# The joint between an embedding gate and the next block's mixer, rearranged by halves of the tokens

## What is computed

```python
# end of the first block: gate by an embedding, then the block's last norm
gate = jax.nn.sigmoid(rms_norm(x, norm_ple) @ w_ple_gate)
x = x + gate * (p @ w_ple_proj)
x = rms_norm(x, norm_final)                       # x * rsqrt(mean(x*x) + 1e-6) * norm_final
# begin of the second block: its norm, modulated, and its mixer's projections
h = rms_norm_2(x, pre_mix_g) * (1.0 + sc1) + sh1
proj = h @ w_in                                   # first the attention's q (4 stripes), k, v
```

## Time and profile before

| | |
|---|---|
| median of 3 runs | 2946.78 us |
| the profiled execution | 2942.8 us, span 2941.0 us |
| TensorE busy | 2821.1 us, 96% |
| VectorE, ScalarE, GpSimd busy | 45%, 31%, 27% |
| mean granted TensorE clock | 0.988 |

### The profile page before, as it was taken

The page is one execution under the profiler, slowest core; times in us unless marked ns, Lnnn a source line. Parts: engine busy times, 40 slices in busy tenths (PEclk is TensorE's granted clock), DMA queues, the critical chain, the costliest instruction groups (busy, mean ns, idle before and its releaser), DMA issues.

```text
span 2941.0 us, 31529 instructions
## 1 busy us (share of the span) xinstructions
PE 2821.1 (96%) x12846; PEld 2261.9 (77%) x12846; DVE 1309.8 (45%) x1448; ACT 916.1 (31%) x1467; POOL 802.1 (27%) x428
## 2 busy tenths in 40 slices
PE   8999999999999999999999999888999999999996
PEld 6666678887788888888877777677767888888885
DVE  6777642231434434432443545326364343444436
ACT  6666421121311111111254233356352312222223
POOL 2433422223212221222243211123431222121224
PEclk9999999999999999999999999999999999999998
DMA  3000011122123222221112101011321111111113
GB/s 113 22 22 9 22 47 53 48 73 79 71 86 116 93 86 100 95 78 51 57 50 94 60 29 36 29 54 58 115 83 47 50 51 49 44 44 50 51 46 126
DMA packets 60864, 182.90 MB, mean 62 GB/s; under 512 B 6473, under 2 KB 15913, under 8 KB 60593
## 3 DMA queue, kind: packets, MB, share of 16 engines
q1 hardware_dynamic: 60720, 180.89, 17.8%
HBM read 165.61 MB, written 15.25 MB: 61 GB/s over the span
## 4 chain that ended last, share of the span: by engine, by line
PE 82%; DVE 5%; ACT 5%; issue 4%; POOL 2%; DMA 2%; SPq 0%; DVEq 0%; POOLq 0%; ACTq 0%
PE psum_mem L543 65%; PE psum_mem L579 2%; PE psum_mem L837 1%; PE psum_mem L842 1%; PE psum_mem L839 1%; PE psum_mem L614 1%; POOL w_lo L2833 1%; PE psum_mem L617 1%; PE psum_mem L615 1%; PE psum_mem L901 1%; PE psum_mem L1066 1%; PE psum_mem L643 1%; DVE left L2060 1%; PE psum_mem L867 1%; ACT w_hi L1203 1%
## 5 line engine op out<-in xcount | busy, mean ns | idle before, releaser
L2833 POOL TENSOR_TENSOR w_lo<-w_raw,w_hi 128x1024 fp32r<-128x1024 f32 (+1 forms) x233 | 549.0, 2357 | 1795.4 <-ACT w_hi L1203 1795.4
L543 PE MATMUL psum_mem<-h_hi,w_hi 128*128 128x512 f32 x2192 | 685.3, 394 | 23.2 <-DVE h_lo L1944 14.0
L543 PE MATMUL psum_mem<-h_hi,w_lo 128*128 128x512 f32 x2192 | 679.7, 391 | 12.0 <-POOL w_lo L2833 12.0
L543 PE MATMUL psum_mem<-h_lo,w_hi 128*128 128x512 f32 x2192 | 678.2, 391 | 0.0
L543 PEld LDWEIGHTS psum_mem<-h_hi,w_hi 128*128 128x128 f32 x2192 | 412.3, 189 | 115.7 <-issue 25.3
L543 PEld LDWEIGHTS psum_mem<-h_hi,w_lo 128*128 128x128 f32 x2192 | 412.3, 189 | 103.5 <-POOL w_lo L2833 18.0
L543 PEld LDWEIGHTS psum_mem<-h_lo,w_hi 128*128 128x128 f32 x2192 | 413.9, 189 | 87.6
L1203 ACT CAST w_hi<-w_raw 128x1024 fp32r<-128x1024 f32 (+1 forms) x233 | 234.0, 1005 | 658.2 <-PE psum_mem L543 511.4
L1949 DVE TENSOR_TENSOR tmp_mem<-psum_mem,norm_row 128x1024 f32<-128x1024 f32 x46 | 56.2, 1225 | 295.3 <-PE psum_mem L543 295.2
L2266 DVE TENSOR_TENSOR x_block<-x_block,psum_mem 128x1024 f32<-128x1024 f32 x88 | 107.4, 1220 | 67.7 <-PE psum_mem L543 65.1
L2876 POOL TENSOR_TENSOR beta<-beta,left 128x128 f32<-128x128 f32 (+2 forms) x96 | 86.8, 905 | 143.5 <-DVE left L2060 141.5
(11 more groups left out here) (355 smaller groups left out, 4006.7 us busy)
## 6 DMA issues: line engine op xcount, KB each, us to landing
ada_raw<-in_w_ada SPq DMA_DIRECT2D x48, 512.0 KB, 4.5
w_raw<-in_w_up_b SPq DMA_DIRECT2D x44, 512.0 KB, 3.3
w_raw<-in_w_in_a SPq DMA_DIRECT2D x32, 512.0 KB, 3.2
w_raw<-in_w_ffn_gate SPq DMA_DIRECT2D x22, 512.0 KB, 3.6
w_raw<-in_w_ffn_up SPq DMA_DIRECT2D x22, 512.0 KB, 3.6
w_raw<-in_w_ffn_down SPq DMA_DIRECT2D x22, 512.0 KB, 4.7
w_raw<-in_w_down_b SPq DMA_DIRECT2D x22, 512.0 KB, 3.2
w_raw<-in_w_in_b_ml SPq DMA_DIRECT2D x16, 512.0 KB, 4.1
```

The costliest lines, as they stand in the source:

```text
L543: made = e.matmul(pairs.half(use, half), wt, x[:, half_of(half)], start=at == 0 and part == 0, stop=at == len(rhs) - 1 and part == 2, skip ...
L2833: e.tensor_tensor(w_lo[:, i, 0:width], w_raw[:, i, 0:width], w_hi[:, i, 0:width].bitcast(F32), ALU.subtract).then_inc(*S.of("w_lo", c))
```

## The change

- Gate rows 0 to 5 stay as they are, but for "next" the squares are scaled by a new column, `final_gain` = sqrt(norm_final^2 + 1e-6), made by ScalarE (3 instructions on 128x8) and VectorE (4 such). So one sum serves both norms, and the step that joined two sums is gone. The plain sum is still made, for a later stage.
- Gate rows 6 and 7 run half by half: row 6 half 0, row 7 half 0, row 6 half 1, row 7 half 1. Everything behind them (scaling, sigmoid, embedding, add, square) is on 128x512 tiles.
- The sum for "next" is made in PSUM: three matmuls with ones for each half add `row2` (rows 0 to 5) and the squares of rows 6 and 7 up. Two of half 0's stand within row 6 half 1, the third behind it. Half 1's stand behind row 7 half 1, ahead of the projections.
- The finished norm is written to PSUM, over its sum, and read from there.
- `mix2` (normed row, `h_hi`, `h_lo`) is made for half 0 and then half 1, and `qk_at` 0 and 1 run over half 0 and then half 1, with `qk_at` 1 two groups behind.
- The fillers on constants (162 matmuls) are gone.
- The plain squares of rows 6 and 7 are made by ScalarE among half 1's `h_hi`, and added by VectorE after its last `h_lo`. SyncE stores `x1` 6 and 7 after three more weight loads instead of between them, and `plain_row` when that late sum is there.

```diff
+            def add_up(use, half, row, first, last):      # was further down, as was halved()
+                made = e.matmul(pairs.half(use, half), const("ones"), row[:, half_of(half)], start=first, stop=last, ...)
 # TensorE
-            for m in range(KD):
+            for m in range(6):
 ...
-            sum_partitions("next", row2, (("inv_m", ("next", 1)),), ("row_v", ("next", "both")), CLOCK_NORM)
+            ends = [take("w_pg") for _ in range(2)]
+            for m in (6, 7):
+                for _ in halved(("pg", m), ends[m - 6], 0, ple_half):
+                    pass
+            row = halved(("pg", 6), ends[0], 1, ple_half)
+            for at in range(KD):
+                next(row)
+                if at == 4:
+                    w.wait_ge("row_g", ("next", 5))
+                    add_up(sum_next, 0, row2, True, False)
+                    w.wait_ge("square", ("next", 6, 0))
+                    add_up(sum_next, 0, gate_sq[0], False, False)
+            w.wait_ge("square", ("next", 7, 0))
+            add_up(sum_next, 0, gate_sq[1], False, True)
+            for _ in halved(("pg", 7), ends[1], 1, ple_half):
+                pass
+            add_up(sum_next, 1, row2, True, False)
+            for m in (6, 7):
+                w.wait_ge("square", ("next", m, 1))
+                add_up(sum_next, 1, gate_sq[m - 6], False, m == 7)
-            two(("w_qk_at", "w_qk_at"), (("qk_at", 0), ("qk_at", 1)), h_rhs("mix2"),
-                ((("rope_in", 0),), (("rope_in", 1),)), CLOCK_NORM + 5)
+            for half in range(NH):
+                steps = [halved(use, n, half, ...) for use, n in firsts]
+                for k in range(KD):
+                    next(steps[0])
+                    if k >= 2:
+                        next(steps[1])
 ...
 # ScalarE
-            ahead(2)
-            w.wait_ge("row_v", ("final", 7))
-            inverse("next", row2, tmp[:, 1, :], eps=1)
+            unit()
+            for m in (6, 7):
+                gate_row(m, 0)
+                gate_square(m, 0)
+            logarithms()
+            inverse_half("next", 0, row2, gate_sq[0], 1)
+            unit()
+            gate_row(6, 1)
+            mix_row(0, 0)
+            gate_square(6, 1)
+            mix_row(1, 0)
             ahead(2)
+            gate_row(7, 1)
+            mix_row(2, 0)
+            gate_square(7, 1)
+            logarithms()
+            mix_row(3, 0)
+            inverse_half("next", 1, row2, gate_sq[0], 1)
+            for k in range(4, KD):
+                mix_row(k, 0)
             for k in range(KD):
+                mix_row(k, 1)
+                if k < 2:
+                    square("final", 6 + k, gate_sq[2 + k][:, :], x1[:, 6 + k, :])
 # VectorE
-            inverse("next", row2, tmp[:, 1, :], eps=EPS * EPS)
-            normed_to_h("mix2", x1, row2, lambda k: gain[:, k:k + 1], lambda k: mod[:, k:k + 1])
+            for m in (6, 7):
+                gate_scaled(m, 0)
+                gate_row(m, 0)
+            gate_scaled(6, 1)
+            inverse_half("next", 0, row2, gate_sq[0], EPS * EPS)
+            mix_normed(0, 0)
+            gate_row(6, 1)
+            mix_normed(1, 0)
+            mix_low(0, 0)
+            gate_scaled(7, 1)
+            mix_normed(2, 0)
+            mix_low(1, 0)
+            gate_row(7, 1)
+            for k in range(3, KD):
+                mix_normed(k, 0)
+                mix_low(k - 1, 0)
+            mix_low(KD - 1, 0)
+            inverse_half("next", 1, row2, gate_sq[0], EPS * EPS)
+            for k in range(KD):
+                mix_normed(k, 1)
+                if k > 0:
+                    mix_low(k - 1, 1)
+            mix_low(KD - 1, 1)
+            for m in (6, 7):
+                w.wait_ge("square", ("final", m))
+                e.tensor_tensor(plain_row[:, :], plain_row[:, :], gate_sq[m - 4][:, :], ALU.add)...
 # SyncE
-            for m in range(KD):
+            for m in range(6):
                 if m % 4 == 0:
                     unit()
                 unit()
+                park(m)
+            unit()
+            unit()
             ahead(2)
+            park(6)
+            park(7)
             unit(2)
             w.wait_ge("row_v", ("final", 7))
             e.dma_start(io["row_park"], plain_row[:, :])...
```

More of the change, by code:

```diff
@@ L575, in sum_partitions, with halved @@
                              skip_group_check=True).then_inc(*S.of("sum", (stage, half)))
+            def halved(use, n, half, rhs, blocks=range(KD)):
+                i, cols = n % 2, half_of(half)
+                for at, b in enumerate(blocks):
+                    high, low = w_hi[:, i, block_of(b)], w_lo[:, i, block_of(b)]
+                    x_high, x_low, events = rhs(at, half)
+                    for event in events:
+                        w.wait_ge(*event)
+                    for part, (wt, x) in enumerate(((high, x_high), (high, x_low), (low, x_high))):
+                        w.wait_ge("w_lo" if part == 2 else "w_hi", n)
+                        made = e.matmul(pairs.half(use, half), wt, x[:, cols], start=at == 0 and part == 0,
+                                        stop=at == KD - 1 and part == 2, skip_group_check=True)
+                    if at == KD - 1:
+                        made.then_inc(*S.of("full", use + (half,)))
+                    yield
+                unit_end[n] = ("full", use + (half,))
+            def add_up(use, half, row, first, last):
+                made = e.matmul(pairs.half(use, half), const("ones"), row[:, half_of(half)], start=first, stop=last,
+                                skip_group_check=True)
+                if last:
+                    made.then_inc(*S.of("sum", (use[1], half)))
             def turn(out, in_, rows=P):
@@ L792, in rotate @@
                 made.then_inc(*S.of("full", use))
-            two(("w_qk_at", "w_qk_at"), (("qk_at", 0), ("qk_at", 1)), h_rhs("mix2"),
-                ((("rope_in", 0),), (("rope_in", 1),)), CLOCK_NORM + 5)
+            h_mix2 = [(h_hi[:, k, :], h_lo[:, k, :],
+                       (("h_hi", ("mix2", k, 1)), ("h_lo", ("mix2", k, 1)))) for k in range(KD)]
+            firsts = [(("qk_at", s), take("w_qk_at")) for s in range(2)]
+            for use, _ in firsts:
+                for event in pairs.take(use, (("rope_in", use[1]),)):
+                    w.wait_ge(*event)
+            for half in range(NH):
+                steps = [halved(use, n, half, lambda k, half: (
+                    h_hi[:, k, :], h_lo[:, k, :],
+                    (("h_hi", ("mix2", k, half)), ("h_lo", ("mix2", k, half))))) for use, n in firsts]
+                for k in range(KD):
+                    next(steps[0])
+                    if k >= 2:
+                        next(steps[1])
+                for s in steps:
+                    for _ in s:
+                        pass
             for s in range(2, 5):
@@ L1053, in tensor @@
                     sum_partitions("plain", plain_back, (("inv_m", ("plain", 1)),))
[L1056 to L1078, removed]
             ends = [take("w_out2") for _ in range(2)]
@@ L1464, in scalar @@
                     inverse("ple", norm_row, tmp[:, 0, :])
+                    square_c, root_c, half_c, gain_c = (final_gain[:, i, :] for i in range(4))
+                    w.wait_ge("final_gain", "square")
+                    e.activation(root_c, square_c, ACT.Ln, bias=eps_col[:, 0:1], scale=1.0).then_inc(*S.of("final_inv", "ln"))
+                    w.own("inv")
+                    e.activation(root_c, root_c, ACT.Exp, bias=0.0, scale=-0.5).then_inc(*S.of("final_inv", "exp"))
+                    w.own("inv")
+                    e.activation(half_c, root_c, ACT.Square, bias=0.0, scale=0.5 ** 0.5).then_inc(*S.of("final_inv", "square"))
                 unit()
@@ L2288, in vector @@
                             ALU.mult).then_inc(*S.of("gain", "all"))
+            square_c, root_c, half_c, gain_c = (final_gain[:, i, :] for i in range(4))
+            e.tensor_tensor(square_c, vec("norm_final", 0, KD), vec("norm_final", 0, KD),
+                            ALU.mult).then_inc(*S.of("final_gain", "square"))
             w.own("gain")
@@ new lines, in mix_normed, with mix_low @@
+            def mix_normed(k, half):
+                cols = half_of(half)
+                w.own("x1")
+                if k >= 2:
+                    w.own("h_lo")
+                e.scalar_tensor_tensor(out=tmp[:, k % 2, cols], in0=x1[:, k, cols], scalar=gain[:, k:k + 1],
+                                       in1=pairs.half(("sum", "next"), half), op0=ALU.mult,
+                                       op1=ALU.mult).then_inc(*S.of("normed", ("mix2", k, half)))
+            def mix_low(k, half):
+                cols = half_of(half)
+                w.wait_ge("h_hi", ("mix2", k, half))
+                e.scalar_tensor_tensor(out=h_lo[:, k, cols], in0=tmp[:, k % 2, cols], scalar=mod[:, k:k + 1],
+                                       in1=h_hi[:, k, cols].bitcast(F32), op0=ALU.add,
```

(6 more changed lines are left out.)

155 lines of the change are left out of this document (93 added, 62 removed).

## The result

| | before | changed |
|---|---|---|
| median | 2945.13 us (20 runs) | 2952.19 us (20 runs) |
| lowest to highest | 2939.78 to 2949.59 | 2948.76 to 2957.84 |
| ratio, 95% interval | | 1.0024 (1.0018 to 1.0031) |
| profiled execution | 2942.8, span 2941.0 | 2948.84, span 2947.1 |

The change costs 7.1 us, where the prediction had 4.9 and a range of 2944 to 2958. It lies above the 0.2% (5.9 us) that I had set as the bound of "no change", so the case that I held likeliest, within 0.2%, didn't come, though the interval reaches down to 0.18%; rival B's size did come. That the measured 2952.19 lies so near the 2951.7 of the prediction is luck: the kernel before measured 1.65 lower here than in the three runs that I had added to, and that hides most of the 2.2 by which the difference was too small.

What follows compares the result with a forecast made beforehand. TensorE, busy 96%, was taken as the bound except at the joint's serial norm. Mark +1.5, first pause +1.8 and third pause +1.6 made 4.9 us longer, 2951.7 on the median; range 2944 to 2958.

Steps and rivals of the forecast that it cites:

- rival B: Slower beyond 0.2%: two low-clock stretches after each of two pauses, +1.5 + 3.2 + 3.2 = 7.9, 2954.7; chance 0.20.
- Row 7's weights: Before row 7's first half: late weights leave TensorE still 4.1 us, then 2.0 us more for `w_lo`.
- First low stretch: After the pause at row 7's first half: clock falls to 1.2 GHz, one stretch and a little, 1.8 us.
- To the second sum: Row 7 half 1 to the second sum: VectorE's half steps of 0.69 to 0.75 set it, sum at 1616.0.
- Second pause "absorbed": Wait of some 4 us before the second sum: its low clock costs nothing, since VectorE feeds the projections.
- The store in the open: Behind the last `h_lo`: adds, `plain_row`'s store, then `late_consts` delay the rotation to 1645.7, 1.5 us later than before.
- Third low stretch: After the pause before the first rotation: one low-clock stretch on a TensorE that is the bound, 1.6 us.
- Row 0's cover of `final_gain`: Gate row 0: its 48 matmuls hide the seven small instructions, cost 0; without the cover at most 2.1.
- the mark: The first rotation's start, 1644.2 before; its shift measures the joint's gain or loss, predicted +1.5 without the clock terms.
- Rival A: The clock stays at its high level in both pauses that count: +1.5, 2948.3; chance 0.16.
- C: Not slower: TensorE's end, not the store, bounds the joint; rotation at 1641.9, -2.3, 2944.5; chance 0.08.
- D: ScalarE pauses at each table switch, up to 1.4 more at each of two loads, 2.8 in all, 2954.5; chance 0.02.

Runs made afterwards that it cites:

- the repair: Changed kernel with row 7's weights loaded, rounded and split before row 5's store, sigmoid and sums: -0.6 us against before, ratio 0.9996.
- the run with half the fillers: Changed kernel with 16, 26 and 16 fillers put back into its three pauses: +1.6 us against before, ratio 1.0010.
- the last run: Changed kernel with row 7's weights early, tables ahead of the store, rounding moved, 18 fillers before the last squares: -8.9 us against before, ratio 0.9973.

## Why the prediction came out as it did

The mechanism was right in its main steps (late weights, a store in the open, low clock behind the pauses), and the sum 4.9 was too small against 7.1. What it lacked was a VectorE held by GpSimd. Its steps:

- **Row 7's weights** (predicted pauses 4.1 and 2.0): 3.5 and 1.7. Right, and the largest loss, since the repair gives 7.7 us of time.
- **First low stretch** (predicted 1.8): the clock was low for 6.8 us. The first sum began its Ln 29.6 us after row 5's scaling; without that stretch I had it at 26.9, which is where the run with half the fillers has it. So the stretch cost 2.7. Too small by 0.9.
- **To the second sum** ("half steps of 0.69 to 0.75"): this step failed. The last `h_lo` came 66.9 us after row 5's scaling where my working had 61.5 plus 1.8, that is 3.6 too late. 0.9 of it is the step above. 2.1 is the one `h_lo` of 2.83, which the moved rounding shows, and 0.6 is row 6's multiply of 1.33 instead of 0.69 beside the split before; it stands on the same chain, but no run took it away by itself. I had priced GpSimd's weight splits as hidden and not asked what VectorE does beside them. The Trainium skill had the rule: by the page "SBUF — State Buffer", section "Who interferes with whom", a VectorE instruction with two inputs in SBUF contends with a GpSimd instruction that reads SBUF, and the port pair that they share is an exclusive lock. The traces agree: 2.83 beside the split and 0.75 without it, while steps with one input in PSUM kept their 0.69 to 0.75 beside a split (0.75 at 1607.12). Worked out by the rule it would be the rest of the split, 2.28, and 0.75 behind it, 3.03, a little above the 2.83 seen.
- **Second pause "absorbed"**: right. The ones-matmul that ends the pause ran at the low clock and took 2.07, but it ends 0.1 us after ScalarE's table load and `h_hi`, which stand ahead of the second Ln anyway. The fillers gained 0.2 us there, and nothing in the last run.
- **The store in the open** (last `h_lo` to rotation 8.1): 7.6. Right. It takes the gain of the projections by halves and more.
- **Third low stretch** (predicted 1.6): 3.1, two stretches instead of one. That it was two is in part chance of the profile: behind a pause as long two other runs had one, which cost 1.8.
- **Row 0's cover of `final_gain`** (priced at 0): right by the trace. From VectorE's last refinement step to its scaling of gate row 0 it is 4.4 us in both kernels. One of the small steps took 2.35 us instead of 0.17, held by GpSimd's split of 1501.28 to 1503.67 in the same way, and was hidden:

```profile
1501.34 2.35 DVE L2403 SCALAR_TENSOR_TENSOR final_gain<-final_gain 128x8 f32<-128x8 f32 x1
```

In my steps the mark was to shift by 3.3 (with the first stretch). It shifted by 6.4: 3.6 more to the last `h_lo`, 0.5 less after it. With the third stretch 3.1 instead of 1.6 the joint is 9.5 longer. One sign that I had named fails: the projections' first matmul was to come 4 to 6 us earlier, and it came 45.3 us after row 5's scaling where it was 46.1 before, 0.8 earlier. The working also has a slip: 1624.0, 1.4, 0.8 and 8 x 1.45 make 1637.8 and not 1637.6, which changes nothing here. Rival A (clock stays high) is refuted by the windows, C (bound by TensorE's end) by the wait of 3.98 for `late_consts`, and D by the table loads, which again had ScalarE's next step directly behind (a load at 1606.59 for 1.28, the sigmoid at 1607.88). Rival B's size came, partly by its own cause and partly by another: two low stretches behind each of the two pauses, as it said (5.8 where it had 6.4), plus a held VectorE that no rival had.

## What to carry to other kernels

When a stage is cut in halves, its inputs are wanted in another order: move the loads, roundings and splits of the second row with it, and everything that was hidden behind the old wait (here a store that later loads stand behind). Price each repair alone before judging the idea: the change as it stood lost 7 us, and with three steps of preparation moved it gains 9. Ask of each VectorE step with two inputs in SBUF what GpSimd does beside it: the profile shows such a step as a long instruction with no wait. A filler should be checked by its records: with twice too many of them nothing of the clock's cost of 5.8 us was to be seen.

## What the runs showed of the hardware

- VectorE's `h_lo` on 128x512 (two inputs in SBUF) took 2.83 us beside a GpSimd subtraction of 2.35 us that had begun 0.07 us earlier, and 0.75 alone. A multiply of 0.69 us took 1.33 beside such a subtraction, and a step on 128x8, where its neighbour of the same size took 0.17, took 2.35.
- After pauses of 3.5 and 1.7 us with two matmuls between, of 1.5 and 5.6, and of 4.0 us, the granted clock was 0.50 for 6.8, 10.2 and 6.8 us; after 2.3 us before the change it was 3.4 us. The length of the pause doesn't fix the length of the stretch. With row 7's weights early, pauses of 1.5 and 5.6 us had 6.8 us at 0.50, and one of 4.0 had 3.4. A pause of 1.85 in row 6 was followed by 3.4 us at 0.50 in the run with the rounding moved, one of 1.81 by none in the changed kernel.
- A float32 matmul on 128 columns makes two records of 0.114 us.
